# One weight stream for the three up projections of the latent attention, and the key's rotation on GpSimd

## What is computed

```python
a = h @ w_a                                     # 1024 -> 384 + 256 + 64
cq, ckv, kr = jnp.split(a, [Q_LORA, Q_LORA + KV_LORA], axis=-1)
q = (rms_norm(cq, g_q) @ w_uq).reshape(B, S, 8, 128 + 64)
q_nope, q_rope = q[..., :128], apply_rope(q[..., 128:], cos, sin)
kv = (rms_norm(ckv, g_kv) @ w_ukv).reshape(B, S, 8, 128 + 128)
k_nope, v = kv[..., :128], kv[..., 128:]
k_rope = apply_rope(kr, cos, sin)
s = (einsum(q_nope, k_nope) + einsum(q_rope, k_rope)) * scale
p = softmax(where(mask, s, -inf))
y = concat_heads(p @ v) @ w_o
```

## Time and profile before

| | before |
|---|---|
| median of three runs | 996.48 us |
| the profiled execution | 997.45 us |
| its span | 995.4 us |
| TensorE busy | 964.8 us |
| VectorE busy | 718.5 us |
| ScalarE busy | 541.4 us |
| GpSimd busy | 17.4 us |
| mean granted TensorE clock | 0.997 |

### The profile page before, as it was taken

The page is one execution under the profiler, slowest core; times in us unless marked ns, Lnnn a source line. Parts: engine busy times, 40 slices in busy tenths (PEclk is TensorE's granted clock), DMA queues, the critical chain, the costliest instruction groups (busy, mean ns, idle before and its releaser), DMA issues.

```text
span 995.4 us, 18903 instructions
## 1 busy us (share of the span) xinstructions
PE 964.8 (97%) x7999; PEld 928.9 (93%) x7999; DVE 718.5 (72%) x1270; ACT 541.4 (54%) x837; POOL 17.4 (2%) x48
## 2 busy tenths in 40 slices
PE   5989999999999999999999999999999999999997
PEld 5978999999998988899999998898999999999996
DVE  5965687887647877699876888656564879888653
ACT  6635564454436556664544545547755567666542
POOL 0000000000000000000000000000130000000000
PEclk9999999999999999999999999999999999999999
DMA  7433467576763742438675894543333545545521
GB/s 285 182 127 112 185 223 269 228 253 255 265 212 134 279 142 114 171 148 318 252 262 206 319 316 170 200 181 128 127 128 127 208 158 189 208 174 207 208 90 43
DMA packets 28307, 194.19 MB, mean 195 GB/s; under 512 B 3264, under 2 KB 3520, under 8 KB 5312
## 3 DMA queue, kind: packets, MB, share of 16 engines
q1 hardware_dynamic: 28224, 192.99, 52.9%
HBM read 191.93 MB, written 1.05 MB: 194 GB/s over the span
## 4 chain that ended last, share of the span: by engine, by line
PE 85%; DVE 7%; ACT 5%; issue 1%; DMA 1%; SPq 1%; POOL 0%; DVEq 0%; ACTq 0%
PE bank L493 24%; PE bank L494 23%; PE bank L499 22%; DVE s_wlo L1350 3%; PE bank L631 2%; PE bank L657 2%; PE bank L554 2%; ACT s_whi L891 2%; PE bank L548 1%; PE bank L513 1%; PE bank L549 1%; PE bank L520 1%; PE bank L514 1%; PE bank L641 1%; DMA s_raw<-in_wa 1%
## 5 line engine op out<-in xcount | busy, mean ns | idle before, releaser
L1350 DVE TENSOR_TENSOR s_wlo<-s_raw,s_whi 128x512 fp32r<-128x512 f32 (+1 forms) x364 | 371.4, 1061 | 142.8 <-ACT s_whi L891 142.4
L891 ACT ACTIVATE s_whi<-s_raw 128x1024 fp32r<-128x1024 f32 (+2 forms) x233 | 305.3, 1336 | 219.0 <-PE bank L499 204.9
L493 PE MATMUL bank<-s_hh,s_whi 128*128 128x256 f32 x1400 | 393.7, 281 | 0.5 <-DVE s_hl L1441 0.2
L494 PE MATMUL bank<-s_hl,s_whi 128*128 128x256 f32 x1400 | 387.7, 277 | 0.0
L499 PE MATMUL bank<-s_hh,s_wlo 128*128 128x256 f32 x1383 | 382.9, 277 | 0.0
L493 PEld LDWEIGHTS bank<-s_hh,s_whi 128*128 128x128 f32 x1400 | 263.2, 188 | 6.2 <-issue 5.1
L494 PEld LDWEIGHTS bank<-s_hl,s_whi 128*128 128x128 f32 x1400 | 263.4, 188 | 0.1
L499 PEld LDWEIGHTS bank<-s_hh,s_wlo 128*128 128x128 f32 x1383 | 259.7, 188 | 0.0
L493 PE MATMUL bank<-s_ph,s_whi 128*128 128x256 f32 x528 | 146.4, 277 | 0.0
L494 PE MATMUL bank<-s_pl,s_whi 128*128 128x256 f32 x528 | 145.8, 276 | 0.0
L499 PE MATMUL bank<-s_ph,s_wlo 128*128 128x256 f32 x516 | 142.5, 276 | 0.0
(11 more groups left out here) (239 smaller groups left out, 1289.6 us busy)
## 6 DMA issues: line engine op xcount, KB each, us to landing
s_raw<-in_gu SPq DMA_DIRECT2D x44, 1024.0 KB, 4.9
s_raw<-in_dn SPq DMA_DIRECT2D x33, 1024.0 KB, 4.9
s_raw<-in_wada SPq DMA_DIRECT2D x24, 1024.0 KB, 5.5
s_raw<-in_up SPq DMA_DIRECT2D x22, 1024.0 KB, 4.9
s_raw<-in_wo SPq DMA_DIRECT2D x8, 1024.0 KB, 4.9
s_raw<-in_win_g SPq DMA_DIRECT2D x8, 1024.0 KB, 4.9
s_raw<-in_wkv_v SPq DMA_DIRECT2D x4, 1024.0 KB, 5.5
s_raw<-in_wkv_k SPq DMA_DIRECT2D x4, 1024.0 KB, 4.7
```

Of the source, the lines that this page charges most:

```text
L493: e.matmul(out, hi, xh[:, k, :], start=first, stop=False, skip_group_check=True)
L494: e.matmul(out, hi, xl[:, k, :], start=False, stop=False, skip_group_check=True)
L891: e.activation(whi[w % SPLIT][:, at], raw[p % RAW][:, at], ACT.Copy).then_inc(S.hi.tick((w, c0)), 1)
L1350: e.tensor_tensor(wlo[s][:, at], raw[p % RAW][:, at], whi[s][:, at].bitcast(F32), ALU.subtract).then_inc(S.lo.tick((i, j), (i, "all")), 1)
```

## The change

It does three things.

1. **One stream.** `wuk`, `wuq` and `wuv` are no longer three arrays with pieces of their own. The list `MLA` names 68 tiles in the order of their use: 4 of `wuk`, 12 of `wuq`, 4 of `wuk`, 12 of `wuq`, all 16 of `wuv`, 4 of `wuk`, 6 of `wuq`, 4 of `wuk`, 6 of `wuq`. Before and after, these are five pieces, the last of 4 tiles. `_order0` takes the units in that order, and `wuk` 4 to 15 move into the list. Banks are handed out anew.
2. **Earlier scores.** `PAIR0` lets `scores 0` come in the middle of the query tiles, ahead of `wuv`; it came behind 16 query tiles and 6 of the 8 units of `wuv`. `PACE0` and `AFTER0` set other paces and distances.
3. **The key's rotation.** Its six operations are issued by GpSimd, ahead of its wait for the bias, with `tmp[0]` and `tmp[1]` as intermediates; the scores wait for a new semaphore.

The diff, cut to its core:

```diff
-STREAM = [("wa", 56), ("wuk", 16), ("wuq", 16), ("wuv", 16), ("wuq", 20), ("wo0", 64), ...
+MLA = ([("wuk", i) for i in range(4)] + [("wuq", i) for i in range(12)] +
+       [("wuk", i) for i in range(4, 8)] + ...
+MLA_AT = {unit: i for i, unit in enumerate(MLA)}
+STREAM = [("wa", 56), ("mla", 68), ("wo0", 64), ...
...
+PACE0 = {"wuk": 0.72, "wuq": 0.84, "wuv": 0.2, "wo0": 0.26}
+PAIR0 = (18, 18, 44, 44)
...
 def _order0():
-    units = _units("wuq")[:16] + [("wuv", g) for g in range(8)] + _units("wuq")[16:] + _units("wo0")
-    return _mixed(units, _soft_steps(range(4)), {"wuq": 0.3, "wuv": 0.6, "wo0": 0.3},
-                  lambda p: ("wuq", (17, 29, 35)[p - 1]) if p else ("wuv", 0), "wo0", 2)
+    units = [(name, i // 2 if name == "wuv" else i) for name, i in MLA[4:] if name != "wuv" or i % 2 == 0] + _units("wo0")
+    return _mixed(units, _soft_steps(range(4)), PACE0, lambda p: units[PAIR0[p]], "wo0", 2, AFTER0)
...
             tiles("wuk", 0, 2, 2, cqh, cql, "cq", 4, S.dve_out)
             sums("kv", 6, columns=True)
-            tiles("wuk", 2, 2, 2, cqh, cql, "cq", 5, S.dve_out)
-            sums("q", 7)
-            for n in (4, 6):
-                tiles("wuk", n, 2, 2, cqh, cql, "cq", (0, 1)[n // 2 - 2], S.dve_out)
...
             for step, i in _order0():
-                if step == "wuq":
+                if step == "wuk":
+                    n, k = i // 2, i % 2
+                    if n % 2 == 0 and k == 0:
+                        bank_of["wuk", n] = (4, 0, 1, 3)[n // 2]
+                        take(bank_of["wuk", n], S.dve_out, ("wuk", n))
...
                     n, k = i // 3, i % 3
+                    if i == 3:
+                        sums("q", 7)
                     if n % 2 == 0 and k == 0:
-                        bank_of["wuq", n] = (2, 3, 0, 1, 2, 3)[n // 2]
+                        bank_of["wuq", n] = (2, 3, 1, 2, 0, 2)[n // 2]
...
-                    q.wait_ge(S.rot, "k")
+                    q.wait_ge(S.rot_k, "k")
...
             low_rank(6, 5, 1)
-            q.wait_ge(S.dve_out, ("cq", 6))
-            rotate(tmp[3][:, :], tmp[4][:, :], A0.K[:, 8, :], A0.K[:, 9, :], "k")
             lo_all(_used_up("wa", 48) + SPLIT)
-            for n in (0, 2, 4, 6):
-                scaled_out("wuk", n, 2, Rs[1], "kv", lambda m: A0.K[:, m, :])
-                if n == 2:
-                    lo_all(_used_up("wa", 56) + SPLIT)
+            lo_all(_used_up("wa", 56) + SPLIT)
+            scaled_out("wuk", 0, 2, Rs[1], "kv", lambda m: A0.K[:, m, :])
...
+            q.wait_ge(S.trig, "cos")
+            q.wait_ge(S.dve_out, ("cq", 6))
+            e.tensor_tensor(tmp[0][:, :], tmp[4][:, :], sinb, ALU.mult)
+            e.tensor_tensor(tmp[1][:, :], tmp[3][:, :], sinb, ALU.mult)
+            e.tensor_tensor(A0.K[:, 8, :], tmp[3][:, :], cosb, ALU.mult)
+            e.tensor_tensor(A0.K[:, 9, :], tmp[4][:, :], cosb, ALU.mult).then_inc(S.rot_k.tick("products"), 1)
+            q.wait_ge(S.rot_k, "products")
+            e.tensor_tensor(A0.K[:, 8, :], A0.K[:, 8, :], tmp[0][:, :], ALU.subtract)
+            e.tensor_tensor(A0.K[:, 9, :], A0.K[:, 9, :], tmp[1][:, :], ALU.add).then_inc(S.rot_k.tick("k"), 1)
             q.wait_ge(S.relb_in, "relb")
```

More of the change, by code:

```diff
@@ L41 @@
 NFIRST = 9
-STREAM = [("wa", 56), ("wuk", 16), ("wuq", 16), ("wuv", 16), ("wuq", 20), ("wo0", 64), ("gu0", 352), ("dn0", 176),
+MLA = ([("wuk", i) for i in range(4)] + [("wuq", i) for i in range(12)] +
+       [("wuk", i) for i in range(4, 8)] + [("wuq", i) for i in range(12, 24)] + [("wuv", i) for i in range(16)] +
+       [("wuk", i) for i in range(8, 12)] + [("wuq", i) for i in range(24, 30)] +
+       [("wuk", i) for i in range(12, 16)] + [("wuq", i) for i in range(30, 36)])
+MLA_AT = {unit: i for i, unit in enumerate(MLA)}
+STREAM = [("wa", 56), ("mla", 68), ("wo0", 64), ("gu0", 352), ("dn0", 176),
           ("wkv_v", 64), ("wkv_k", 64), ("wq1", 64), ("wo1", 64), ("gu1", 352), ("dn1", 176),
@@ L138, in _stick_steps, with _mixed @@
             yield "keep", p
-def _mixed(units, steps, paces, pair_at, chunk_name, per=1):
+def _mixed(units, steps, paces, pair_at, chunk_name, per=1, after=AFTER):
     steps, ahead, at, made, credit = iter(steps), [], {}, set(), 0.0
@@ L159, in ready @@
         else:
-            need, tiles = (AFTER[name][0], i), AFTER[name][1]
+            need, tiles = (after[name][0], i), after[name][1]
         return need in at and n >= at[need] + tiles
@@ L185, in _mixed, with _mla_used @@
         yield taken(len(units))
+def _mla_used(step, i):
+    return _used_up("mla", MLA_AT[step, 2 * i if step == "wuv" else i])
+PACE0 = {"wuk": 0.72, "wuq": 0.84, "wuv": 0.2, "wo0": 0.26}
+PAIR0 = (18, 18, 44, 44)
+AFTER0 = {**AFTER, "exp": ("scores", 9), "scale": ("exp", 3), "values": ("turn1", 7), "chunk": ("values", 0)}
 def _units(name):
@@ L690, in tensor_program @@
             for step, i in _order0():
-                if step == "wuq":
+                if step == "wuk":
[3 more added lines that the diff above has]
+                        take(bank_of["wuk", n], S.dve_out, ("wuk", n))
+                    q.wait_ge(S.xlo, ("cq", k))
+                    product("wuk", i, banks[bank_of["wuk", n - n % 2]][:, (n % 2) * T:(n % 2 + 1) * T], cqh, cql, k,
+                            k == 0, k == 1, ("wuk", n - 1) if n % 2 == 1 and k == 1 else None)
+                elif step == "wuq":
                     n, k = i // 3, i % 3
+                    if i == 3:
+                        sums("q", 7)
                     if n % 2 == 0 and k == 0:
-                        bank_of["wuq", n] = (2, 3, 0, 1, 2, 3)[n // 2]
+                        bank_of["wuq", n] = (2, 3, 1, 2, 0, 2)[n // 2]
                         take(bank_of["wuq", n], S.dve_out, ("wuq", n))
@@ L1046, in scalar_program @@
             rms("q")
+            hi_all(_used_up("mla", 0) + SPLIT)
             scale0 = float(192.0 ** -0.5)
             for step, i in _order0():
-                if step == "wuq":
-                    if i % 4 == 0:
-                        hi_part(_used_up("wuq", i) + SPLIT)
+                if step in ("wuk", "wuq"):
+                    if MLA_AT[step, i] % 4 == 0:
+                        hi_part(_mla_used(step, i) + SPLIT)
                 elif step == "wuv":
                     if i % 2 == 0:
-                        hi_part(_used_up("wuv", 2 * i) + SPLIT)
+                        hi_part(_mla_used(step, i) + SPLIT)
                     if i % 4 == 3:
@@ L1556, in vector_program @@
             low_rank(6, 5, 1)
[L1557 to L1558 removed]
             lo_all(_used_up("wa", 48) + SPLIT)
[L1560 to L1563 removed]
+            lo_all(_used_up("wa", 56) + SPLIT)
+            scaled_out("wuk", 0, 2, Rs[1], "kv", lambda m: A0.K[:, m, :])
             for step, i in _order0():
                 if step == "wuv":
[L1567 removed]
+                    lo_part(_mla_used(step, i) + SPLIT)
+                elif step == "wuk":
+                    if i % 4 == 3:
+                        scaled_out("wuk", i // 4 * 2, 2, Rs[1], "kv", lambda m: A0.K[:, m, :])
+                    if i % 2 == 1:
+                        lo_part(_mla_used(step, i) + SPLIT)
                 elif step == "wuq":
[L1569 to L1570 removed]
+                    if i % 2 == 1 and i % 6 != 5:
+                        lo_part(_mla_used(step, i) + SPLIT)
                     if i % 6 == 5:
@@ L1577, in vector_program @@
                             rotate(A0.Q[:, 8 + c, :], A0.Q[:, 10 + c, :], A0.Q[:, 8 + c, :], A0.Q[:, 10 + c, :], ("q", c))
+                        lo_part(_mla_used(step, i) + SPLIT)
                 elif step == "wo0":
                     if i == 0:
-                        lo_all(_used_up("wuq", 36) + SPLIT)
+                        lo_all(_used_up("mla", 68) + SPLIT)
                     if i % 2 == 1:
```

25 lines of the change are left out of this document (14 added, 11 removed).

## The result

| | before | changed |
|---|---|---|
| median | 996.63 us (994.83 to 997.64, 4 runs) | 991.25 us (990.85 to 991.77, 4 runs) |
| the profiled execution | 997.45 us | 991.77 us |
| its span | 995.4 us | 989.5 us |
| TensorE busy | 964.8 us | 962.8 us |
| GpSimd busy | 17.4 us | 25.5 us |

The account below looks back on a forecast made before the run. TensorE, busy 964.8 of 995.4 us, was taken as the bound. Gains 5.94 + 1.7 − 0.58 − 0.1 = 7.0 us, less 2.9 for collisions, gave 4.0; 993.4, less 0.97 for the median, made 992.5 us, range 989.0 to 996.5.

Parts of the forecast that it names:

- What was to be had, 7.6 us: Stage from 36 to 110 us: five TensorE waits lose 5.94 us and the slow clock 1.7 us, no more to gain.
- Term 1: First scores: TensorE arrives at 45.5 us, undisturbed VectorE's chain ends at 45.49, so zero wait but no slack.
- Term 2: GpSimd's six key-rotation steps all collide with VectorE's low halves, delaying the first scores by 2.9 us (bounds 1.5 and 4.4).
- The price of one step: VectorE's loss per 256-column GpSimd step, taken as two passes, 0.49 us; one pass would be 0.24 us.
- Term 3: Later waits vanish except 0.58 us of 2.04 at the first output-projection tile; no clock fall; 0.1 us for changing product kinds.
- No collision: Rival, chance 0.18: GpSimd's rotation does not slow VectorE, so the 7.0 us come in full, 989.5 us.
- The lock for the whole instruction: Rival, chance 0.13: GpSimd's fixed part also blocks VectorE, 6 x 0.66 = 3.9 us; gain 3.1 us, 993.4 us.
- The clock falls at the new wait: Rival, chance 0.11: first scores some 2.9 us late make the clock fall, taking back 1.7 us; 994.2 us.
- A later wait: Rival, chance 0.10: `turn 2a` waits for the mask of scores 3; lateness of 3 us leaves 1.0 gained, 995.5 us.
- GpSimd as the bound: Rival, chance 0.06: scores 0 wait for GpSimd's rotation; at 3.5 us a step the kernel takes 1001.2 us.

## Why the prediction was right, and where it was off

The direction was right, 991.25 us is in the range, 1.2 below the forecast, and the waits and collisions of its terms are in the trace. Two sizes were off, and the share of the clock fitted the medians by luck.

- **What was to be had, 7.6 us.** Right for the profiled execution: all of the difference lies in this stage, the clock is at 1.00 from 36 to 110 us, and the fall cost 1.6 us where 1.7 was said. But the 1.7 was one execution's fall. With the 0.97 us taken off for the median, the forecast gave the clock 0.7 us there; over 51 executions it is 996.12 − 995.25 = 0.9. That is luck, since one trace doesn't say how often the clock falls.
- **Term 1.** TensorE arrives at 45.46 us, forecast 45.5. VectorE had no slack, as said. Its chain began 0.49 us earlier (35.65, not 36.14). In five more traces of this order it began at 35.35 to 35.95 us, so the start varies; whether the change has a part in it is open. The wait for a high half, 0.35 us, came with it: this half was ready at 38.4 us, and a chain that began at 36.14 would have wanted it at 38.55, "in time".
- **Term 2, the mis-sized one.** "All six collide, 6 x 0.49 = 2.9 us" failed in the count, less in the price. Four steps collide with low halves: the first, held off through four of them, costs the fifth 0.20, and the next three cost 1.23 − 0.68 = 0.55 us each, 1.84 us together. The last two steps ran beside evictions from banks and cost nothing. With VectorE's pause the low halves take 2.2 us more than alone, and so they do with hardly a pause, in the run with eight steps. So 2.2 stands against the 2.9, and less the 0.49 of the earlier start 1.7 came to TensorE. The low halves take 7.0 us with the pause, not 7.7, and GpSimd is at it for 8.2 us, not 6.5.
- **The price of one step.** It was worked out from a select of 128 columns by a pass count. It measured 0.55 us in a low half and 0.41 to 0.54 in the queries' rotation. The Trainium skill (SBUF — State Buffer, SBUF: two separate sides) has the two exclude each other for the whole instruction, and the one that starts first has the way. Our rows agree that a low half waits for a GpSimd step with two inputs, but for 0.55 of the 0.75 us that it takes alone; and they differ on who goes first, since GpSimd's first step began ahead of three low halves (35.89 against 36.25 us and later) and waited for all of them. The estimate from the Trainium skill's page GPSIMD Engine Reference, 3.1, was 0.56 us, and was nearer than mine; by it and six collisions the forecast would have been 0.4 us higher still, since the count was wrong.
- **Term 3.** As forecast: no wait at scores 1, scores 2, `turn 2a` or chunk 1, 0.42 us shown at the first output tile where 0.4 was said. The run without its cover brought 1.79 back. That its absence also keeps the clock up isn't shown: of three traces with this wait of 1.79 us, one has the fall. The 0.1 us for one more change of kinds wasn't seen.
- **The rivals.** *No collision* fell: VectorE loses 1.84 us. It is nearly what happens in the kernel before with the move alone, 0.47 us. *The lock for the whole instruction* named 3.9 us and fell on size. *The clock falls at the new wait* didn't happen in the two traces of the changed kernel (waits of 1.54 and 1.55 us), nor, by a mean clock of 0.998 or more, in six of its seven other executions. It did in the three traces where this wait was 1.87, 2.06 and 2.81 us, and took 4.8, 3.2 and 1.5 us between scores 0 and scores 1, where 1.7 was forecast. One of the three kernels is the changed one up to there, line for line. So it stood closer than its 0.11 told. *A later wait* and *GpSimd as the bound* fell: the key was ready at 44.05 us, 3.1 ahead of the scores.
- **What the forecast didn't see.** That four low halves on VectorE's chain, those of the `wuv` piece, are not needed for the first scores, and that without them the whole loss there goes. Moving them is worth 1.5 to 1.8 us more at the medians and makes GpSimd's part needless. The version with them moved and the rotation on VectorE is the best settled one, 989.48 us, 6.4 less than before by its ratio.

The forecast's 4.0 us and the 5.87 by which the stage got shorter differ by 1.2 at the first scores (0.7 from the size of term 2, 0.5 from the earlier start), 0.1 from the change of kinds, and some 0.6 of small terms of which half stays open.

## What to carry to other kernels

Walk the releaser's chain back from the wait and ask of every operation on it whether the waiting product needs it: here it was worth 1.5 to 1.8 us to move four operations that only a later product needs, and 0.2 us of the chain to move six to an idle engine. Work that is given to GpSimd isn't free for VectorE if both read SBUF twice: place it beside evictions from banks, or count half a microsecond per 256-column step. And count a fall of the clock as a cost with a chance, in the time before as in the time after: it shows in some executions only, so compare executions in which the clock held before you credit a change with it.

## What the runs showed of the hardware that I had not expected

- **A run of VectorE operations on SBUF can hold GpSimd off whole.** Three steps of 0.74 to 0.75 us took 2.85, 3.08 and 2.35 us in the kernel before with the move alone, and each low half beside them took its 0.68 us. In the changed kernel the first step too waited for four low halves, but then VectorE went on with four more behind a pause of 0.35 us, and the two alternated for the next 4 us. No long pause is needed for that: in the run with eight steps they alternated just so behind a pause of 0.02 us, at the same low half. In all of these traces the first step ended 0.6 us behind the end of the fourth low half, and what differs is what VectorE did then. Why GpSimd gets its turn there and not between the earlier ones isn't tested.
- **Evictions from banks with one SBUF input are not slowed.** Pairs of them took 0.74 and 0.75 us with and without a GpSimd step beside them.
- **The clock.** In this stage it fell to 1.2 GHz at waits of 1.87, 2.06 and 2.81 us in the traces shown and not at 1.54 and 1.55. At 1.79 us it fell in the trace of before, and not in those of two other kernels. But the length of the wait isn't all: it also fell near 610 us in one trace, where TensorE had been idle for 0.82 us, and near 17 us in just the three traces that fell at scores 0. These three kernels, with ten executions each, have 4.2 to 4.9 us between their fastest and slowest, the others of the changed kernel's kind, with four or five, 0.1 to 1.6, and the version with no wait at all, with six, 2.9 (mean clocks from 0.995 to 0.998, no fall in its trace). So a fall doesn't need a wait in this stage, and what decides it stays open.
